# Attention products on 64 rows of the array, a two-pass gate input, and other tables in a decoder layer on one core

## What is computed

```python
proj = rmsnorm(x) @ w_in                # u_a, u_gate, q, k, v, g_out, gk_low
conv_out = conformer_conv(u_a, u_gate)  # GLU, causal depthwise conv of 31 taps, LayerNorm, swish
gk = log_sigmoid(gk_low @ gk_w + gk_b) / 16       # rank 16
b = cumsum(gk)  # in chunks of 64 tokens; 4 heads of 64 key and 128 value channels
q_t, k_t, k_s = q * exp(b) / 8, k * exp(-b), k * exp(b_last - b)
scores = where(causal, q_t @ k_t.T, 0)            # inside a chunk
o = scores @ v + q_t @ state
state = state * exp(b_last) + k_s.T @ v           # chunk after chunk
x = x + concat(conv_out, headnorm(o) * silu(g_out)) @ w_out
x = x + hier_moe(rmsnorm(x))     # best of 4 groups, best 2 of its 8 experts, SwiGLU of width 512
return rmsnorm(x)
```

## Time and profile before

| what | value |
|---|---|
| median of 3 runs | 1132.62 us (1126.9 to 1134.95) |
| profiled execution | 1127.82 us, span of its instructions 1126.1 us |
| granted clock, mean | 0.973 |
| busy: PE, DVE, ACT, POOL | 1061.4, 930.5, 697.1, 465.3 us |
| chain that ended last | PE 27%, DMA 24%, DVE 7%, ACT 3% |

### The profile page before, as it was taken

One profiled execution on the slowest core, in us unless ns is written; L12 is line 12 of the kernel. 1 busy time (PEld: TensorE's weight loads), 2 busy tenths in 40 slices (PEclk: granted clock), 3 DMA queues, 4 the chain that ended last, 5 costly groups with the idle time before them and its releaser, 6 DMA issues.

```text
span 1126.1 us, 14945 instructions
## 1 busy us (share of the span) xinstructions
PE 1061.4 (94%) x5033; PEld 852.9 (76%) x5033; DVE 930.5 (83%) x879; ACT 697.1 (62%) x695; POOL 465.3 (41%) x377
## 2 busy tenths in 40 slices
PE   7999999999999986899999999999999999999980
PEld 5758888877788865788888888888888787888860
DVE  5479999784666676799999999998998999999963
ACT  6675464433731232577777777777787778777753
POOL 0277998621200001334243433434454556454434
PEclk9999999999999996899999999999999999999995
DMA  9421110200532245599999999999999999999927
GB/s 327 134 76 38 38 57 19 75 1 1 188 131 95 111 168 200 196 355 378 358 385 384 359 403 389 379 374 383 372 371 364 355 378 347 385 353 370 356 99 299
DMA packets 69494, 283.04 MB, mean 251 GB/s; under 512 B 12896, under 2 KB 31520, under 8 KB 42576
## 3 DMA queue, kind: packets, MB, share of 16 engines
q1 hardware_dynamic: 53232, 251.75, 58.9%
q0 software_dynamic: 11664, 18.11, 6.6%
q10 hardware_dynamic: 4560, 12.67, 2.8%
HBM read 271.47 MB, written 30.94 MB: 269 GB/s over the span
## 4 chain that ended last, share of the span: by engine, by line
PE 27%; DMA 24%; DVE 7%; ACT 3%; issue 2%; SPq 0%; POOL 0%; POOLq 0%; ACTq 0%; DVEq 0%
DMA raw<-in_expert_w_gate_dram 16%; PE ps L1906 8%; PE ps L1904 8%; PE ps L1905 8%; DVE w_lo L1507 4%; DMA raw<-in_expert_w_up_dram 4%; ACT w_hi L1040 3%; DMA summed_rows<-ym,now_s 2%; DMA raw<-summed_rows 1%; PE ps L1897 1%; DMA hf_rows<-hfp 1%; PE ps L1926 1%; DVE hfp L1362 0%; PE ps L1822 0%; SPq L555 0%
## 5 line engine op out<-in xcount | busy, mean ns | idle before, releaser
L1507 DVE TENSOR_TENSOR w_lo<-raw,w_hi 128x2048 fp32r<-128x2048 f32 x206 | 468.2, 2291 | 45.9 <-ACT w_hi L1040 42.1
L1040 ACT ACTIVATE w_hi<-raw 128x2048 fp32r<-128x2048 f32 x206 | 393.5, 1917 | 88.4 <-DMA raw<-in_expert_w_up_dram 36.4
L1904 PE MATMUL ps<-w_hi,xm_hi 128*128 128x512 f32 x560 | 224.5, 401 | 3.0 <-DVE xm_lo L1520 1.7
L1906 PE MATMUL ps<-w_hi,xm_lo 128*128 128x512 f32 x560 | 222.7, 398 | 0.0
L1905 PE MATMUL ps<-w_lo,xm_hi 128*128 128x512 f32 x560 | 221.9, 396 | 0.0
L1904 PEld LDWEIGHTS ps<-w_hi,xm_hi 128*128 128x128 f32 x560 | 105.4, 188 | 29.7 <-DVE w_lo L1507 1.9
L1905 PEld LDWEIGHTS ps<-w_lo,xm_hi 128*128 128x128 f32 x560 | 105.9, 189 | 25.0
L707 POOL DMA_INDIRECT summed_rows<-ym,now_s x35 | 115.6, 3302 | 21.2 <-issue 20.6
L1906 PEld LDWEIGHTS ps<-w_hi,xm_lo 128*128 128x128 f32 x560 | 105.6, 189 | 24.1
L1904 PE MATMUL ps<-w_hi,hm_hi 128*128 128x512 f32 x280 | 113.1, 404 | 1.9 <-DVE hm_lo L1533 1.6
L1906 PE MATMUL ps<-w_hi,hm_lo 128*128 128x512 f32 x280 | 111.3, 398 | 0.0
(11 more groups left out here) (316 smaller groups left out, 1986.5 us busy)
## 6 DMA issues: line engine op xcount, KB each, us to landing
raw<-in_expert_w_down_dram SPq DMA_DIRECT2D x70, 1024.0 KB
raw<-in_expert_w_up_dram SPq DMA_DIRECT2D x69, 1024.0 KB
raw<-in_expert_w_gate_dram SPq DMA_DIRECT2D x68, 1024.0 KB
raw<-in_w_in_dram SPq DMA_DIRECT2D x8, 1024.0 KB
xa<-in_x_dram SPq DMA_DIRECT2D x8, 512.0 KB, 8.5
raw<-in_w_out_dram SPq DMA_DIRECT2D x4, 1024.0 KB
xin<-in_x_dram SPq DMA_DIRECT2D x8, 512.0 KB, 3.4
hf_rows<-hfp ACTq DMA_DIRECT2D x8, 512.0 KB, 2.6
```

What stands on the lines that cost most here:

```text
L1040: act.activation(w_hi[:, slot, :], raw[:, r, :], ACT.Copy).then_inc(hi_rdy, 1)
L1507: dve.tensor_tensor(w_lo[:, slot, :], raw[:, r, :], w_hi[:, slot, :].bitcast(F32), ALU.subtract)\
L1904: pe.matmul(dst, x_hi, w_hi[:, s, cols], start=first, stop=False)
L1906: return pe.matmul(dst, x_lo, w_hi[:, s, cols], start=False, stop=stop)
```

## The change

Low-rank gate input: high and low part of the 16 weight columns lie side by side (wl, 32 columns). Each block is multiplied twice: with the input's high part and with its low part. The 32 resulting rows go into lowT, and gk_w lies twice in gkw, so that the next product adds both halves. This adds the product of low by low part.

Scores: four products of 64 rows and 128 columns for a tile, the heads of even number into bank 3, the odd into bank 5. The mask takes two instructions. Keys times values: the same eight products with 64 rows each, chunk 0 into bank 5, chunk 1 into bank 3, in an order that takes the chunks of a head one after the other. As both products now use both banks, scores wait for the state of the tile before, and keys times values for the mask of their own tile.

Tables: oneR and jcol in fp32r. table(5) comes after the last product of the output projection instead of ahead of the logits of tile 6.

The wait for the stored rows leaves VectorE; SyncE has one ahead of the loads of expert 0's down weights.

```diff
@@ SyncE, after load_second(0), load_second(1)
+            for b in range(2):
+                sp.wait_ge(hf_out[b], 16 * (NT // 2))
             load_first(4)
             load_first(5)
@@ ScalarE
-            act.dma_start(gkw[:], gk_w[0]).then_inc(low_in, 16)
+            for r in range(2):
+                act.dma_start(gkw[r * RANK:(r + 1) * RANK, :], gk_w[0]).then_inc(low_in, 16)
@@ VectorE, masked(t)
-                dve.copy_predicated(ssb[:, t % 2, :], cmask[:].bitcast(I32), ps[:, 3, :]).then_inc(ssb_rdy, 1)
+                for r in range(2):
+                    heads = (v.rearrange("p (q r i) -> p q r i", q=PAIRS, r=2)[:, :, r, :]
+                             for v in (ssb[:, t % 2, :], cmask[:].bitcast(I32)))
+                    last = dve.copy_predicated(*heads, head_scores(r).rearrange("p (q i) -> p q i", q=PAIRS))
+                last.then_inc(ssb_rdy, 1)
@@ VectorE, before the indices
-            dve.wait_ge(hf_out[0], 16 * (NT // 2))
-            dve.wait_ge(hf_out[1], 16 * (NT // 2))
             dve.wait_ge(oh_used, 2 * NT)
@@ TensorE, projections
-                    pe.matmul(dst, w_h[:, k, :], x_l, start=False, stop=False)
-                    last = pe.matmul(dst, w_l[:, k, :], x_h, start=False, stop=(k == K_ORDER[-1]))
+                    last = pe.matmul(dst, w_h[:, k, :], x_l, start=False, stop=(w_l is None and k == K_ORDER[-1]))
+                    if w_l is not None:
+                        last = pe.matmul(dst, w_l[:, k, :], x_h, start=False, stop=(k == K_ORDER[-1]))
@@ TensorE, keys_scores(t)
                     pe.wait_ge(ssb_rdy, t)
+                    pe.wait_ge(st_rdy, 2 * t)
                 for pr in range(PAIRS):
-                    last = pe.matmul(ps[:, 3, pr * 2 * P:(pr + 1) * 2 * P].rearrange("p (h i) -> p h i", h=2),
-                                     kT[:, pr, tok], qz[:, 2 * pr:2 * pr + 2, tok], start=True, stop=True)
+                    for r in range(2):
+                        rows_h = slice(r * HK, (r + 1) * HK)
+                        last = pe.matmul(head_scores(r)[:, pr * P:(pr + 1) * P], kT[rows_h, pr, tok], qz[rows_h, 2 * pr + r, tok],
+                                         start=True, stop=True)
@@ TensorE, keys_values(t)
-                if t:
-                    pe.wait_ge(st_rdy, 2 * t)
-                for c in range(2):
-                    for h in range(HEADS):
-                        rows_h = slice(h % 2 * HK, (h % 2 + 1) * HK)
-                        last = pe.matmul(ps[rows_h, 5, (2 * c + h // 2) * HV:(2 * c + h // 2 + 1) * HV],
-                                         kz[:, c, h * HK:(h + 1) * HK], x2[:, t, h * HV:(h + 1) * HV],
+                pe.wait_ge(ssb_rdy, t + 1)
+                for h in range(HEADS):
+                    rows_h = slice(h % 2 * HK, (h % 2 + 1) * HK)
+                    for c in range(2):
+                        rows_c = slice(c * CH, (c + 1) * CH)
+                        last = pe.matmul(chunk_values(c)[rows_h, h // 2 * HV:(h // 2 + 1) * HV],
+                                         kz[rows_c, c, h * HK:(h + 1) * HK], x2[rows_c, t, h * HV:(h + 1) * HV],
                                          start=True, stop=True, skip_group_check=True)
@@ TensorE, tile t of the output projection
-                if t >= 2:
+                if 2 <= t < NT - 1:
                     table(t - 2)
                 logits(t - 1)
                 if t == NT - 1:
                     out_projection(t, 1, range(2, KC))
+            table(NT - 3)
             ranks(NT - 2)
```

More of the change, by code:

```diff
@@ L145, in layer_program @@
         dg = at("dg", [P, NT, P], over=o_acc)
-        gkw = at("gkw", [RANK, DK], over=o_acc + 4 * T)
+        gkw = at("gkw", [2 * RANK, DK], over=o_acc + 4 * T)
         w_low = at("w_low", [P, KC, RANK], over=o_acc + 5 * T)
-        wl_lo = at("wl_lo", [P, KC, RANK], F32R, over=o_acc + 5 * T)
-        wl_hi = at("wl_hi", [P, KC, RANK], F32R, over=o_acc + 6 * T)
+        wl = at("wl", [P, KC, 2 * RANK], F32R, over=o_acc + 6 * T)
         rb = at("rb", [P, T], over=o_acc + 8 * T)
@@ L152, in layer_program @@
         scanmask = at("scanmask", [P, T], over=o_kT)
-        lowT = at("lowT", [RANK, T], over=o_kT + 4 * T)
+        lowT = at("lowT", [2 * RANK, T], over=o_kT + 4 * T)
         sq = at("sq", [P, CT, 512], over=o_u + 4 * PIECE)
@@ L203, in layer_program @@
         hfp = at("hfp", [P, 2, D], over=o_q + 4 * D)
-        oneR = at("oneR", [P, 2, CAP], over=o_q + 12 * D)
-        jcol = at("jcol", [P, 2, NC, NE], over=o_q + 13 * D)
+        oneR = at("oneR", [P, 2, CAP], F32R, over=o_q + 12 * D)
+        jcol = at("jcol", [P, 2, NC, NE], F32R, over=o_q + 13 * D)
         w_first = at("w_first", [P, 3, PIECE], over=o_xn)
@@ L243, in wide, with head_scores, chunk_values @@
             return ps[:, n:n + 2, :].rearrange("p b n -> p (b n)")
+        def head_scores(r):
+            return ps[:, 3 + 2 * r, r * 2 * P:(r + 1) * 2 * P]
+        def chunk_values(c):
+            return ps[:, 5 - 2 * c, c * 2 * HV:(c + 1) * 2 * HV]
         def sem(name):
@@ L786, in _ @@
                     .then_inc(xkh_rdy, 1)
-            act.wait_ge(low_in, 32)
-            act.activation(wl_hi[:], w_low[:], ACT.Copy).then_inc(ph_rdy, 1)
+            act.wait_ge(low_in, 48)
+            act.activation(wl[:, :, 0:RANK], w_low[:], ACT.Copy).then_inc(ph_rdy, 1)
             for i in range(NT):
@@ L1156, in weights_lo @@
                 if p == "low":
-                    ins = dve.tensor_tensor(wl_lo[:], w_low[:], wl_hi[:].bitcast(F32), ALU.subtract)
+                    ins = dve.tensor_tensor(wl[:, :, RANK:], w_low[:], wl[:, :, 0:RANK].bitcast(F32), ALU.subtract)
                 else:
@@ L1222, in _ @@
                     dve.wait_ge(tg_ps, n + 1)
-                    dve.tensor_tensor(lowT[:, cols], ps[0:RANK, bank(n), :], rb[0:RANK, cols], ALU.mult).then_inc(tg_dve, 1)
+                    dve.tensor_tensor(lowT[:, cols], ps[0:2 * RANK, bank(n), :], rb[0:2 * RANK, cols], ALU.mult).then_inc(tg_dve, 1)
                     conv(4 if h else 12)
@@ L1325, in state @@
                             st[:, (n + 1) % 4, pr, :], st[:, n % 4, pr, :], dec[:, pr, n:n + 1],
-                            ps[:, 5, (2 * c + pr) * HV:(2 * c + pr + 1) * HV], ALU.mult, ALU.add)
+                            chunk_values(c)[:, pr * HV:(pr + 1) * HV], ALU.mult, ALU.add)
                     last.then_inc(st_rdy, 1)
@@ L1633, in _ @@
             last.then_inc(rb_ps, 1)
-            pe.wait_ge(low_in, 32)
+            pe.wait_ge(low_in, 48)
             def value_product(t):
@@ L1656, in _ @@
                 cols, tiles = slice(h * 512, (h + 1) * 512), half_tiles(h)
-                m = RANK if what == "low" else P
+                m = 2 * RANK if what == "low" else P
                 if what == "gk":
@@ L1664, in _ @@
                     pe.wait_ge(*split_in("low"))
-                    w_h, w_l = wl_hi[:], wl_lo[:]
+                    w_h, w_l = wl[:], None
                 elif n < 8:
```

## The result

| | kernel before | changed kernel | ratio, 95% interval |
|---|---|---|---|
| first measurement, median of 10 and 10 | 1131.2 us | 1124.09 us (1117.58 to 1127.24) | 0.9925 (0.9902 to 0.9948) |
| second measurement, medians of 12 and 6 | 1133.45 us | 1120.54 us (1119.39 to 1124.34) | 0.9891 (0.9861 to 0.9921) |

By the ratios the change takes 8.5 us in the first and 12.4 in the second (the medians differ by 7.1 and 12.9); the intervals overlap, and together they say about 10.

A forecast was written before the change was run, and what follows sets the result against it. TensorE was taken as full in the output projection and experts, with a serial tail between; 0 + 0.9 - 3.1 - 5.9 + 0.3 = -7.8 us gave 1120.0 (profile) or 1124.8 (median), put at 1121.5, range 1114 to 1130.

The forecast's parts named there:

- Order at the end and store wait: Tail after the projection: x2 of tile 7 comes 4.6 us earlier, the last table ends 5.9 us earlier.
- The half clock that I booked behind the projection: Logits of tile 7 may run wholly at half clock after TensorE's next pause: 0.4 us back.
- The contention of loads with the gather: Tail of the later weight loads can meet the first gather: +0.3 us, 2 if it meets it whole.
- Tables: Five one-pass tables (tiles 0 to 4) in the gapless output projection each save 0.62 us: 3.1 us.
- Attention loop: Scores, keys times values and new waits over all tiles: +0.9 us, between -0.5 and +1.8.
- four parts of the array give nothing over two: Keys times values: 8 products at 0.11 us each as before, plus 0.15 for one more change of form.
- The new wait in tile 7: Keys times values waits for the mask uncovered: state +1.25 us, 0.32 formerly idle; first output projection 0.9 later.
- Gate input: Low-rank products: 3.7 us of TensorE go, 1.9 remain after a longer pause, ScalarE's eviction comes no earlier: 0 booked.
- (a): Attention loop: all four array parts work at once, about 4 us more gained, -11.7 us, 1116; chance 0.15.
- (b): Tail: half clock before tile 6's logits, or gather meets loads; 2 to 4 us return, 1123 to 1128; chance 0.18.
- (c): Scores and keys times values: passes on alternate row halves do not overlap, net +30 us, 1150; chance 0.05.
- (d): Tables and tail: one-pass format or order gives nothing, only some -3 us, 1125 to 1130; chance 0.07.

The follow-up runs named there:

- the second profile: The changed kernel run and profiled once more, unaltered: 1120.54 us, ratio 0.9891 to the kernel before; the profiled execution took 1119.39 us.
- end_only: One-pass tables, table 5 last and the moved store wait, in the kernel before: 1121.94 us, ratio 0.9912.
- move_only: Only table 5 moved behind the last product of the output projection, in the kernel before: 1126.96 us, ratio 0.9937.
- spw_only: Only the wait for the stored rows moved from VectorE to SyncE, in the kernel before: 1130.54 us, ratio 0.998.
- kv_order: Changed kernel with keys times values in the other order, all heads of chunk 0 ahead of chunk 1: 1121.16 us, one run.
- warm: Changed kernel with 11 extra products of 512 columns, result overwritten, in TensorE's pause ahead of gk: 1121.8 us, ratio 0.9905.
- best1: Changed kernel with the gate input as before and tile 7's mask ahead of the convolution's scaling: 1121.53 us, ratio 0.9901 to the kernel before.
- no_low: Changed kernel with the gate input as before: 1122.05 us, ratio 0.9892 to the kernel before.
- low_only: The two-pass gate input alone, in the kernel before: 1131.64 us, ratio 0.9995.

## Why the prediction was right and where it was off

**The time.** 1121.5 was forecast, 1124.09 and 1120.54 were measured, both within 1114 to 1130. That the middle value fits so well is in part luck: it lay between two bases that the prediction did not choose between (1120.0 from the profile, 1124.8 from the median), and the two measurements lie 3.6 us apart. The steps gave -7.8 us up to expert 0; the first profile has -5.6 there and the second -10.4. Most of the 2.6 us between the sum and the second profile is one term, the attention loop (2.1); most of what the first profile lacks against the second is the clock.

**Order at the end and store wait (-5.9).** Measured -4.75 to x2 of tile 7 and -0.99 behind it: -5.7 in the second profile and -5.7 in end_only. The division was right too: 4.6 was forecast for x2. In move_only and spw_only each part showed its own share alone. But all this is measured from a profile of the kernel before with a short stretch at half clock: on average over the four profiles with the old order and the ten with the new, x2 of tile 7 comes 5.2 us earlier (18.7 against 13.4). The half clock that I booked behind the projection (0.4 back) did come in the second profile, from 424 us on; choice 7 begins 6.68 us after x2 instead of 6.13, so it took 0.55. The contention of loads with the gather (+0.3) did not: first gather to first expert product takes 7.13 us before and 7.12 in the second profile; only the first profile has 7.75. Half clock is not the reason, since it covers this stretch in all profiles. The gather itself took 5.1 us to land there, and 4.3 to 4.5 in the others that show it. The second down weight was still on its way until 445.4, 3.5 us into the gather, which is the contention that I had booked; but spw_only, where the two overlap by 2.9 us, has 7.13, so the cause stays open.

**Tables (-3.1).** Measured -3.1: 0.62 us for each of five, as worked out from one row of one-pass pitch.

**Attention loop (+0.9, measured -1.15).** This is the step that failed, and it is the reading of keys times values: "four parts of the array give nothing over two". It took 0.60 us for the eight products, not 0.97, and the loop's -1.15 lies outside the -0.5 to +1.8 that I gave it (though under the 2 us that I had named as the sign of being wrong).

Single records of the changed kernel's tile 3 show why: keys times values' 16 passes start in groups of four, 7 ns from one to the next, and the groups 0.109 us apart (247.271, 247.380, 247.489). In the kernel before they start in pairs with the same 0.109. So a slot of 0.109 holds as many passes as the array has parts. I had read the pairs as "a product costs one pass" and carried that to four parts; with two parts both readings give eight slots, and the earlier trace rows could not tell them apart. The single records of the kernel before could have: if only the second pass of a product overlapped the first of the next, the first slot behind a change of form would hold one pass, and it holds two (242.757 and 242.763, the start of L1762). The records do not name the part that a pass used. That each part works through its own passes, whatever their written order, is the reading that fits the pairs, the fours and kv_order alike; it is inferred.

Scores, with two parts, start in pairs 0.112 apart and take 0.65 us, near the forecast of 0.74 (0.86 less 0.12). The price of a changed form came out a little above my 0.15: from scores to masked scores times values the last slot lasts 0.208 and the next first one 0.213 instead of 0.112, together 0.20 more. Per tile all changes of form and the shorter products make -0.30, where I had 0.0. Over eight tiles that would be -2.4; about half arrives.

By the starts of the masks (first profile against the kernel before) the first scores to mask 0 gives 0.3, tile 2 to 3 gives 0.6 (9.45 against 10.04), 5 to 6 gives 0.9 (15.68 against 16.59); the other five steps stay within 0.2, and mask 7 to the projection loses 0.46. In these five VectorE paces: it reaches the mask with next to no idle time, or, from 3 to 4, TensorE waits for its sums of the convolution (1.01 us before, 1.29 after).

**The new wait in tile 7.** Right in place and kind: mask, then products, then state, 0.32 of idle time used up. The state is 0.84 later against the mask instead of 1.25, since the products take 0.60 instead of 1.15 with drain. Moving the mask ahead of the scaling takes it away (88.55 against 89.16 us).

**Gate input (0).** Right in sum, and for the wrong reason. Of the 3.7 us the pause took 1.7, as forecast (2.57 instead of 0.86), and 2.0 remained. I let ScalarE absorb these, and hid the cost in clock behind them. But TensorE runs without a gap from gk to the first scores, so all that it gains or loses there arrives at them, and the longer stretch at half clock takes back what the shorter product sequence gives. ScalarE's eviction only stands close behind: where the scores came earliest (warm, 155.95 us) it came 0.5 us after them, and the step from mask 0 to mask 1 grew by 0.2.

**Rivals.** (a), all four parts at once, was right about the array: keys times values came down as it said (0.60 with the price of the form, 0.44 without), and scores take four slots (0.65 with the price, 0.45 without), which both readings had given. It was wrong in what this is worth: it put the loop some 4 us under the forecast's +0.9, and it came out 2 under, since the changes of form cost and VectorE paces five of the steps. At expert 0 the second profile's -10.4 lies nearer to its -11.7 than to my -7.8, the first profile's -5.6 does not; the times can't tell the two apart. The Trainium skill (TensorEngine Tiling (Array Packing), Tiling Modes) was the better guide here than my reading of the pairs: its four independent tiles are in the trace (7 ns), and so is its drain at a change of form (0.2). (b), half clock in the logits of tile 6 or in the last products behind them, happened in 2 of the 10 profiles that have the new order (the first of the changed kernel, 2.0 us up to x2 and 0.9 up to the index; move_only, 0.4 up to x2), for which 0.18 was a fair chance; it cost less than the 2 to 4 us that I gave it. (c) is out: scores with 64 rows overlap. (d) is out by move_only and by the tables.

**Behind the first index.** The time from expert 0 to the end varies by 5 us between profiles (672.2 to 677.0), in kernels that are the same there: 672.35 before, 674.12 and 675.91 in the two profiles of the changed kernel, 672.9 in best1. TensorE's idle time there, for VectorE, goes with it (5.3 us in the kernel before, 9.1 in no_low, which has the 677.0); ScalarE's waits for the weight loads do not (102.0 us in low_only, with 672.2, and 94.0 in no_low). So one profile's span can't test a change of this size; the medians do, and theirs of about 10 us agree with the 10.4 at expert 0 of the second profile, but not better than their intervals allow. Whether an earlier start of the experts loses a microsecond or so to the loads stays open.

## What to carry to other kernels

Parts of TensorE's array count by position, rows as well as columns: passes in 64 by 64 form started four at once here, so where an operand is padded with zeros to 128 rows, dropping the padding can pay, in whatever order the products come. Count the changes of form against it (0.15 to 0.2 us each here), and expect it only in steps that TensorE paces. Pull short dependent steps (a table, a mask) out from between independent products; here the table gave 4.3 us, more than its wait of 3.31, and the earlier mask 0.6 in the trace. A shortened piece of TensorE's work that only lengthens its next pause may be paid back in clock (it came out even here, and why was not shown), so compare executions by the clock's stretches before trusting one profile's difference.

## What was not expected of the hardware

The half clock behind the same pause is not the same from one execution to the next: 3.4, 6.8 or 10.2 us with 0.86 us of pause, 6.8, 10.2 or 13.7 with 2.57, and 6.8 with none. The same holds for the end of the projection in the new order: half clock began 2.4 to 3.1 us after x2 of tile 7 in eight profiles, and 8.6 and 5.3 us before it in two. A wait that the profile puts down to a DMA (2.0 to 2.4 us) had 1.45 us of TensorE's table beneath it, which showed only once the DMA was no longer waited for.
